# Modulation in small chunks beside the projection, with partial sums kept on chip

## The chip, the cores and the metric

The kernel runs on one core of a Trainium2 chip. The metric is the device time of one execution in microseconds (us). An engine's name and its short form in the profile: TensorE (PE; PEld is its weight load), VectorE (DVE), ScalarE (ACT), GpSimd (POOL), SyncE (SP). A "q" behind it means its instruction queue, for instance where it issues a DMA.

## What is computed

One layer of a decoder trunk, for 256 prompt tokens and 8 x 8 sample tokens, 320 in all, with model width 4096, in 32-bit floats:

```
mod = c @ w_ada + b_ada                      # 4096 x 12288, 9 rows of c
shift, scale, gate = jnp.split(mod, 3, axis=-1)
h = _rmsnorm(x, g_norm) * (1.0 + scale[:, None]) + shift[:, None]
proj = h @ w_in                              # 4096 x 10240
a_b, a_c, a_x, a_g, b_x, b_g, c_u, c_g = _split_cols(proj)
...
mixed = jnp.concatenate([out_a, out_b, out_c], axis=-1) @ w_out   # 4096 x 4096
x = x + gate[:, None] * mixed
```

out_a is a short gated convolution of 1024 channels. out_b (2048 channels) is a convolution of b_x, two gates from small matmuls, a recurrence in time and a gate from b_g. out_c (1024 channels) is a complex diagonal state space model on c_u (S5, in 8 units of 4 tiles), a GLU and a gate from c_g. A final RMSNorm follows. The states after the last token are outputs too.

## The kernel before

Activations lie transposed: 128 channels on the partitions, 320 tokens in the free dimension, 32 such tiles for h. Each large weight comes as slabs of 512 KB. A main slab holds two blocks of 128 rows by 512 columns. SyncE loads it (RAW, a ring of four), ScalarE rounds it to w_hi (L529), VectorE takes the rest, w_lo (L833), and TensorE multiplies: for four column blocks and two row blocks three matmuls with h_hi or h_lo, 24 in all (L375 to L377). A group of 512 output columns fills the four banks of the PSUM tensor M and is then read out. Weights are split three slabs ahead of use (AHEAD).

The modulation product goes the other way round: c (32 columns, 9 of them used) is the stationary operand and a slab of w_ada streams past it. A slab has two matmuls of 512 columns, recorded as four; each goes to another strip of 32 output partitions (r = 32 * (k % 4)). The four strips are partial sums, so ScalarE copies them out (acc_copy), and four matmuls with a selection matrix add them and turn them (ada_sum, L401).

The order of the work is written out by hand, engine by engine, with semaphores:

- First stage. ScalarE loads x whole, then the sum of squares is made (L853, L386). Shift and scale of four chunks of 512 channels follow, 128 modulation slabs from a ring of eight (L393, ada_ring). VectorE makes the normalised and modulated rows h (h_tmp, h_rows), four tiles a chunk.
- Folded stage (N_P = 8 groups of 8 main slabs, the lower half of the contraction). Before every main slab stand two modulation slabs of the other four chunks (ada_ring_x, a ring of four), and an ada_sum behind every eighth. The half sums of six groups go through ScalarE to DRAM (part_b, part_c), those of the last two to SBUF.
- U stage (N_U = 4 groups of 8 slabs): the upper half for c_u and c_g, added on VectorE.
- A stage (8 groups of 16 slabs) for the short convolution; beside it runs the S5 recurrence, on all engines, one unit a group.
- G stage: 8 slabs of the GLU.
- B stage: four times the upper half of b_x (8 slabs), then b_g (16 slabs), with the recurrence beside it (the gates' matmuls at L481).
- O stage: 8 output groups of 16 slabs. Gate modulation is folded in, two slabs after eight of the main slabs of each group (L499), then a sum (L507) behind slab 13. SyncE issues main and gate slabs in turn (L338, L340). At a group's end ScalarE copies out, VectorE adds gate times output to x (L1164 to L1167), ScalarE squares (L804), VectorE adds the squares (L1171).
- Tail: the sum of squares over partitions (L511), root, reciprocal (L1179), x times 1/rms times weight on VectorE (L1184) and, for two of eight groups, GpSimd and ScalarE (L1313, L815); y goes out as 5 MB.

The tables for S5 (T0, 14 rows of 1064) are computed whole on VectorE and ScalarE in the first stage.

## Time and profile before

| | |
|---|---|
| median of three runs | 2138.58 us (2137.79 to 2139.91) |
| the profiled execution | 2137.69 us, its span 2136.1 us |
| TensorE busy, weight load | 94%, 81% |
| VectorE, ScalarE, GpSimd busy | 49%, 37%, 20% |
| DMA | 473.88 MB, 222 GB/s over the span |
| chain that ended last | PE 74%, POOL 7%, DMA 7%, issue 5%, DVE 4% |

The span is the time from the first instruction to the last; what lies around it is in the execution's own time alone. Busy is the time with an instruction under way. Matmuls are pipelined and their ends are modelled, so the distance of starts says what one costs, not its length. A window's row gives the busy time with the number of instructions for PE, PEld, DVE, ACT and POOL in this order, then PEclk, the share of TensorE's full clock that was granted, the busy share of the DMA engines and GB/s. In a timeline's row the bracket tells how long the engine was idle before it and what ended that.

### The profile page before, as it was taken

How to read it: one execution, taken by the hardware profiler on the slowest of the kernel's cores; microseconds unless marked ns; L12 is line 12 of the kernel's file. 1: busy time of each engine (PE TensorE's matmuls, PEld its weight loads, DVE VectorE, ACT ScalarE, POOL GpSimd, SP SyncE). 2: the span in 40 equal slices, each digit the busy share in tenths (PEclk: the TensorE clock that was granted, in tenths of full speed). 3: DMA queues.
4: the chain of work that ended last, by engine and by line, in shares of the span. 5: the costliest groups of instructions: out<-in, count | busy, mean ns of one | idle time of the engine just before them, and what ended most of it. 6: DMA issues, size and time to landing. Idle time of an engine off the chain costs nothing.

```text
span 2136.1 us, 36787 instructions
## 1 busy us (share of the span) xinstructions
PE 2007.3 (94%) x13066; PEld 1724.2 (81%) x13066; DVE 1051.4 (49%) x1324; ACT 800.7 (37%) x1075; POOL 434.3 (20%) x501
## 2 busy tenths in 40 slices
PE   2887999999999998999989999999999999999994
PEld 0111777778999997989979999999988888888883
DVE  4812233233447677676777455565653333333334
ACT  3001223233334444444435445646563323333232
POOL 0000000000107765867658101000000000000001
PEclk9999999999999999999999999999999999999997
DMA  7999999997543433334333444454457787666862
GB/s 311 410 410 385 334 339 348 344 332 291 172 144 127 133 127 117 129 120 141 123 126 130 161 147 165 134 173 154 155 216 259 261 318 258 249 247 246 306 234 98
DMA packets 129149, 473.88 MB, mean 222 GB/s; under 512 B 14640, under 2 KB 15472, under 8 KB 128960
## 3 DMA queue, kind: packets, MB, share of 16 engines
q1 hardware_dynamic: 122256, 445.70, 58.1%
q0 software_dynamic: 4816, 18.10, 2.5%
q10 hardware_dynamic: 2016, 9.42, 1.1%
q8 instruction: 19, 0.31, 0.1%
q14 instruction: 42, 0.34, 0.1%
HBM read 463.09 MB, written 10.07 MB: 222 GB/s over the span
## 4 chain that ended last, share of the span: by engine, by line
PE 74%; POOL 7%; DMA 7%; issue 5%; DVE 4%; ACTq 1%; ACT 1%; POOLq 0%; SPq 0%; DVEq 0%
PE m L375 22%; PE m L377 21%; PE m L376 21%; DMA ada_ring<-in_ada 6%; PE aux L393 4%; PE aux L499 3%; POOL s_tmpp L1260 1%; POOL s_tmpp L1257 1%; PE aux L481 1%; DVE x L1184 1%; POOL cos L1218 1%; POOL s_h__105 L1256 1%; POOL sin L1216 1%; DMA ada_ring_x<-in_ada 1%; DVE w_lo L833 1%
## 5 line engine op out<-in xcount | busy, mean ns | idle before, releaser
L375 PE MATMUL m<-h_hi,w_hi 128*128 128x320 f32 x3584 | 1131.8, 316 | 4.7 <-DVE w_lo L833 4.6
L377 PE MATMUL m<-h_hi,w_lo 128*128 128x320 f32 x3584 | 1109.4, 310 | 0.0
L376 PE MATMUL m<-h_lo,w_hi 128*128 128x320 f32 x3584 | 1109.0, 309 | 0.0
L833 DVE TENSOR_TENSOR w_lo<-w_raw,w_hi 128x1024 fp32r<-128x1024 f32 x456 | 577.4, 1278 | 838.4 <-ACT w_hi L529 837.3
L529 ACT ACTIVATE w_hi<-w_raw 128x1024 fp32r<-128x1024 f32 x456 | 478.9, 1056 | 903.2 <-PE m L377 577.5
L375 PEld LDWEIGHTS m<-h_hi,w_hi 128*128 128x128 f32 x3584 | 674.9, 188 | 130.9 <-issue 113.6
L376 PEld LDWEIGHTS m<-h_lo,w_hi 128*128 128x128 f32 x3584 | 675.5, 188 | 0.8
L377 PEld LDWEIGHTS m<-h_hi,w_lo 128*128 128x128 f32 x3584 | 675.0, 188 | 0.0
L393 PE MATMUL aux<-ada_ring,c_T 128*32 128x512 f32 x512 | 123.8, 620 | 24.3 <-DMA ada_ring<-in_ada 24.3
L393 PEld LDWEIGHTS aux<-ada_ring,c_T 128*32 128x32 f32 x512 | 17.7, 110 | 124.2 <-DMA ada_ring<-in_ada 120.1
L393 PE MATMUL aux<-ada_ring_x,c_T 128*32 128x512 f32 x512 | 70.8, 612 | 3.6 <-DMA ada_ring_x<-in_ada 3.6
L1226 POOL DMA_DIRECT2D part_b<-part_b x4 | 2.4, 588 | 339.0 <-ACT part_b L605 339.0
L499 PE MATMUL aux<-gate_ring,c_T 128*32 128x512 f32 x512 | 69.2, 605 | 2.0 <-DMA gate_ring<-in_ada 2.0
L1309 POOL DMA_DIRECT2D x<-in_x x8 | 4.2, 531 | 312.9 <-PE m L377 312.9
L1313 POOL TENSOR_TENSOR x<-x,rstd 128x320 f32<-128x320 f32 x8 | 8.6, 1111 | 225.5 <-DVE rstd L1179 225.5
L1300 POOL COPY stage_h<-lru_r 128x18 f32<-128x18 f32 x8 | 4.9, 616 | 240.7 <-DVE lru_r L1094 240.7
L576 ACT ACTIVATE ada_acc<-aux 128x512 f32<-128x512 f32 x16 | 9.5, 595 | 117.0 <-PE aux L393 116.9
L1256 POOL TENSOR_TENSOR s_h__104<-q,cos 128x328 f32<-128x328 f32 x16 | 19.7, 1232 | 156.0 <-DVE q L1007 156.0
L1219 POOL TENSOR_TENSOR sin<-sin,cos 128x328 f32<-128x328 f32 x34 | 45.9, 1349 | 6.0 <-POOL cos L1218 5.9
L628 ACT ACTIVATE cos<-sin 128x328 f32<-128x328 f32 x33 | 15.6, 473 | 68.4 <-POOL sin L1219 68.3
L386 PE MATMUL aux<-x_sqa,sel_ones 128*128 128x320 f32 x8 | 4.6, 757 | 37.4 <-DVE x_sqa L853 37.4
L1260 POOL TENSOR_TENSOR s_tmpp<-q,cos 128x328 f32<-128x328 f32 x32 | 37.8, 1180 | 0.0
(237 smaller groups left out, 1507.6 us busy)
## 6 DMA issues: line engine op xcount, KB each, us to landing
w_raw<-in_w SPq DMA_DIRECT2D x456, 512.0 KB, 4.3
ada_ring<-in_ada SPq DMA_DIRECT2D x128, 512.0 KB, 9.0
ada_ring_x<-in_ada SPq DMA_DIRECT2D x128, 512.0 KB, 5.9
gate_ring<-in_ada SPq DMA_DIRECT2D x128, 512.0 KB, 5.7
x<-in_x ACTq DMA_DIRECT2D x1, 5120.0 KB, 16.6
x<-in_x POOLq DMA_DIRECT2D x8, 640.0 KB, 5.3
out_y<-x SPq DMA_DIRECT2D x7, 640.0 KB, 3.0
part_b<-part_b POOLq DMA_DIRECT2D x4, 688.0 KB, 6.5
```

Source lines behind the costliest of these rows:

```text
L375: mm(out, w_hi, hi[:, k, :], start=k == k0, stop=False)
L376: mm(out, w_hi, lo[:, k, :], start=False, stop=False)
L377: last = mm(out, w_lo, hi[:, k, :], start=False, stop=k == k0 + nk - 1)
L393: last = mm(A0[part][r:r + 32, :], CT[:, k, :], slot[:, kk, :], start=k < 4, stop=k >= KT - 4)
L481: last = mm(A0[2 * w + hd][:, 0:XW], WG[:, 2 * pr + hd, w, :], XB[:, 2 * pr + hd, :], start=True, stop=True)
L499: last = mm(A0[0][r:r + 32, :], CT[:, k, :], ADA2[:, n % RING, kk, :], start=k < 4, stop=k >= KT - 4)
L529: fn(W_HI[:, c % RING], RAW[:, c % RING].rearrange("p (k n) -> p k n", k=2), ACT.Copy).then_inc(w_hi_done, 1)
L833: tt(W_LO[:, c % RING], RAW[:, c % RING].rearrange("p (k n) -> p k n", k=2), W_HI[:, c % RING].bitcast(F32), SUB).then_inc(w_lo_done, 1)
L1184: last = stt(X[:, k, :], X[:, k, :], col(C_GF + k), RST2[:], MUL, MUL)
L1219: tt(sin, sin, cos, SUB).then_inc(frac_done, 1)
L1256: tt(hr, qr, cos, MUL)
L1260: then(tt(TMPP[:], qi, cos, MUL))
```

## The change

The modulation is cut into nine chunks of 32 slabs. Eight hold shift and scale for 512 channels each, the ninth the first quarter of the gate. A slab now is one block of 128 rows by 1024 columns, as four matmuls of 256 columns, one per output strip, all with the same stationary operand (recorded as eight). Each strip holds finished sums, so a VectorE transpose from PSUM takes the place of the copy and the selection matmuls, and the PSUM banks alternate between chunks.

Only chunk 0 stands before the first main slab, and TensorE does 24 of its slabs before the sum of squares. x comes in eight pieces and is kept where h_lo will be. The modulation slabs of the other eight chunks (256) are folded in four at a time behind every second main slab, at places that pairs_after gives: behind n = -3, -1, 1, 3, 4, 6, 8, 10, 11, 13 and so on, eight times in fourteen slabs. Their ring has six slots for the first 32 slabs and then four.

The head is now 14 half groups (seven groups of 512 columns: b_x of three, c_u, c_g) over eight steps of the contraction, 112 slabs of four row blocks by 256 columns. After each slab the sums go from PSUM to SBUF: copied by ScalarE in the first step, added by VectorE in the other seven. b_x of the three groups goes to DRAM at the end of the head and comes back in the B stage, which has 80 slabs instead of 96. The U stage is gone. S5 tables are made in four batches during the first four steps.

In the O stage gate modulation for two groups at a time is folded in, two slabs behind every second main slab, over the first six groups; TensorE waits for gmod_done at the start of groups 0, 2 and 4. ScalarE multiplies x by the final norm's weight after each group. The last group is read from PSUM by VectorE bank by bank, and the final product is ten wide operations on VectorE, with the root's table loaded early by a dummy operation.

```diff
-ADA_J = 8
-ADA_1 = ADA_J // 2
+HC, HK = 256, 4
+HGROUPS, HSTEPS = 7, 8
+HSL = 2 * HGROUPS
+N_H = HSL * HSTEPS
+CHUNKS = 9
+CW = 256
...
+        pairs_after = {n: [q for q in range(128) if (q | 1) * HSL // 16 - 3 == n] for n in range(-3, N_H)}
+
+        def ada_place(n):
+
+            if n < KT:
+                return n % 6, n // 6 + 1, n - 5
+            m = n % RING
+            first = KT + m
+            return m, len(range(m, KT, 6)) + (n - first) // RING + 1, (
+                n - RING + 1 if n >= first + RING else max(range(m, KT, 6)) + 1)
...
+            for n in range(-3, N_H):
+                if n in (HSL - 2, 2 * HSL - 2, 3 * HSL - 2):
+                    s5_batch((n + 2) // HSL)
+                for q in pairs_after[n]:
+                    for m in (KT + RING + 2 * q, KT + RING + 2 * q + 1):
+                        if m < CHUNKS * KT:
+                            ada_in(m)
+                if RING <= n + 6 < N_H:
+                    w_in(n + 6)
...
+            def ada_slab(n, bank):
+
+                slot, landed, _ = ada_place(n)
+                pe.wait_ge(ada_landed[slot], 16 * landed)
+                k = n % KT
+                for r in range(4):
+                    last = mm(A0[bank][32 * r:32 * r + 32, 0:CW], CT[:, k, :], ADAX[slot][:, r, :], start=k == 0,
+                              stop=k == KT - 1)
+                last.then_inc(ada_used, 1)
...
+            def head_slab(n):
+
+                st_, l, s_ = n // HSL, n % HSL, n % RING
+                pe.wait_ge(w_lo_done, n + 1)
+                if l == 0:
+                    pe.wait_ge(h_lo_done, st_ + 1 + 1)
+                if 2 <= n < HSL + 2:
+                    pe.wait_ge(hda_free, n - 2 + 1)
+                if n >= HSL + 2:
+                    pe.wait_ge(hdv_free, n - 2 - HSL + 1)
...
+            pe.wait_ge(c_in, 16)
+            for n in range(24):
+                ada_slab(n, 0)
             pe.wait_ge(sqa_done, 8)
...
+            for n in range(24, KT):
+                ada_slab(n, 0)
+            for n in range(-3, 0):
+                pairs(n)
+            for n in range(N_H):
+                head_slab(n)
+                pairs(n)
...
+            with pe.Fori(0, 3) as p:
+                k = 0
+                pe.wait_ge(gmod_done, p + 1 + 1)
+                for jj in range(2):
+                    for c in group_o(2 * p + jj):
+                        if c not in ((1, 3, 5, 7, 9, 11, 13, 15) if jj else (2, 4, 6, 8, 10, 12, 14, 15)):
+                            continue
...
+            def sums(n):
+
+                dve.wait_ge(slab_done, n + 1 + 1)
...
+                row, few = head_place(n)
+                bk = 2 * (n % 2)
+                tt(row, row, M[:, bk:bk + 2, 0:TP], ADD)
+                tt(few, few, MS[:, bk:bk + 2], ADD).then_inc(hdv_free, 1)
...
+            with dve.Fori(0, 3) as p:
+                st.enter(p, 2)
+                for odd in range(2):
+                    group_o(2 * p + odd, odd, False)
+                dve.wait_ge(gate_used, KT * (p + 1))
+                nc.vector.transpose(MODT2[:].rearrange("p b n -> p (b n)"), A0[0][:, 0:CW]).then_inc(gate_t_done, 1)
+                dve.wait_ge(gate_t_done, p + 1)
+                tt(MODG[:], MODT2[:, :, 0:9], PAR[:, bass.ds(C_BADA + 72 + 8 * p, 8)].unsqueeze(2).to_broadcast(
+                    [P, 8, 9]), ADD).then_inc(gmod_done, 1)
```

## Rows read from the trace of the kernel before

**Rows 1.** Windows by stage: length, busy us (xinstructions), clock, DMA share, GB/s

```profile
0.00:211.27 211.27, 139.46 (x592) 28.39 (x592) 83.94 (x119) 32.41 (x33) 1.45 (x5) 0.98 0.96 380
211.27:519.47 308.20, 308.20 (x2106) 244.06 (x2105) 97.35 (x108) 90.05 (x140) 9.54 (x11) 1.00 0.94 338
519.47:632.45 112.98, 112.98 (x770) 112.71 (x770) 51.43 (x70) 37.51 (x38) 9.37 (x16) 1.00 0.48 165
632.45:1179.10 546.65, 522.97 (x3394) 489.87 (x3392) 385.56 (x514) 247.19 (x372) 377.39 (x407) 0.98 0.38 127
1179.10:1209.97 30.87, 30.86 (x192) 30.87 (x193) 13.17 (x12) 13.62 (x18) 1.08 (x2) 0.93 0.41 143
1209.97:1566.34 356.37, 356.37 (x2371) 350.02 (x2369) 202.25 (x255) 201.99 (x259) 21.87 (x42) 1.00 0.45 153
1566.34:2103.35 537.01, 535.02 (x3650) 467.77 (x3648) 195.12 (x214) 169.45 (x203) 5.00 (x10) 1.00 0.71 256
2103.35:2136.10 32.75, 1.45 (x3) 0.50 (x2) 22.58 (x35) 8.51 (x15) 8.62 (x8) 0.58 0.40 160
```

**Rows 2.** Timeline of TensorE, first stage: start, us, engine, line, what, xcount [idle]

```profile
155.69 1.05 PE L393 MATMUL aux<-ada_ring,c_T 128*32 128x512 f32 x4 [0.23 <-DMA ada_ring<-in_ada]
156.98 1.05 PE L393 MATMUL aux<-ada_ring,c_T 128*32 128x512 f32 x4 [0.24 <-DMA ada_ring<-in_ada]
```

**Rows 3.** Timeline of TensorE, folded stage

```profile
216.19 1.06 PE L393 MATMUL aux<-ada_ring_x,c_T 128*32 128x512 f32 x8
...
220.90 1.07 PE L393 MATMUL aux<-ada_ring_x,c_T 128*32 128x512 f32 x8
```

**Rows 4.** Timeline of TensorE, A stage: matmuls with 32 output columns

```profile
760.51 0.46 PE L457 MATMUL aux<-s_h__104,s_cc 128*32 128x328 f32 x1
...
760.81 0.44 PE L457 MATMUL aux<-s_h__104,s_cc 128*32 128x328 f32 x1
```

**Rows 5.** Timeline of TensorE, start of the kernel

```profile
41.97 4.27 PE L393 MATMUL aux<-ada_ring,c_T 128*32 128x512 f32 x32
...
47.07 1.05 PE L393 MATMUL aux<-ada_ring,c_T 128*32 128x512 f32 x4 [0.83 <-DMA ada_ring<-in_ada]
...
52.35 1.05 PE L393 MATMUL aux<-ada_ring,c_T 128*32 128x512 f32 x4 [0.23 <-DMA ada_ring<-in_ada]
```

**Rows 6.** Timeline of SyncE's queue, same stretch

```profile
43.86 15.19 SPq L303 DMA_DIRECT2D ada_ring<-in_ada  x16
```

**Rows 7.** Timeline of VectorE at the first stage's end

```profile
208.16 1.38 DVE L939 TENSOR_SCALAR h_tmp<-h_tmp,mod 128x256 f32<-128x256 f32 x4
```

**Rows 8.** Timeline of TensorE, folded stage: a sum step, and one long burst

```profile
249.05 0.95 PE L401 MATMUL aux<-sel_ones,ada_acc 128*128 128x9 f32 x8
249.93 1.06 PE L393 MATMUL aux<-ada_ring_x,c_T 128*32 128x512 f32 x8
...
259.35 1.55 PE L393 MATMUL aux<-ada_ring_x,c_T 128*32 128x512 f32 x8
```

**Rows 9.** Groups of instructions by line, VectorE: busy, mean ns, idle before

```profile
L833 DVE TENSOR_TENSOR w_lo<-w_raw,w_hi 128x1024 fp32r<-128x1024 f32 x456 | 577.4, 1278 | 838.4 <-ACT w_hi L529 837.3 <-DVE y_sqs L1149 0.2
...
L853 DVE TENSOR_TENSOR x_sqa<-x_sqa,x_sq 128x1280 f32<-128x1280 f32 x7 | 10.4, 1492 | 1.0 <-ACT x_sq L555 0.3
```

**Rows 10.** Timeline of SyncE's queue at the O stage's start

```profile
1572.03 1.76 SPq L334 DMA_DIRECT2D gate_ring<-in_ada  x4
```

**Rows 11.** Timeline of TensorE, same stretch

```profile
1575.34 1.05 PE L499 MATMUL aux<-gate_ring,c_T 128*32 128x512 f32 x4 [1.80 <-DMA gate_ring<-in_ada]
```

**Rows 12.** Timeline of VectorE at the end of the first output group

```profile
1636.95 1.67 DVE L1164 SCALAR_TENSOR_TENSOR x<-out_tmp,mod,x 128x256 f32 x4 [1.79 <-ACT out_tmp L800]
...
1640.24 2.28 DVE L1171 TENSOR_TENSOR y_sqs<-y_sqs,y_sq 128x320 f32<-128x320 f32 x4 [0.71 <-ACT y_sq L804]
```

**Rows 13.** Timeline of TensorE, tail

```profile
2109.31 1.43 PE L511 MATMUL aux<-y_sqs,sel_ones 128*128 128x320 f32 x2 [5.94 <-DVE y_sqs L1171]
```

**Rows 14.** Timeline of VectorE, tail

```profile
2113.52 16.03 DVE L1184 SCALAR_TENSOR_TENSOR x<-x,par,rstd 128x320 f32<-128x320 f32 x24
```

More of the change, by code:

```diff
@@ L322, in _, with ada_in @@
-            for n in range(RING):
-                sp.wait_ge(ada_used, 2 * first - 2 * RING + n + 1)
-                sp.dma_start(ADAX[:, n], a["ada"][2 * first - RING + n]).then_inc(adax_landed[n], 16)
-            with sp.Fori(N_P * SPH // RING, SLAB_O // RING + 1) as r:
+            sp.sem_inc(bank_free, BLK)
+            def ada_in(n):
+                slot, _, used = ada_place(n)
+                if used > 0:
+                    sp.wait_ge(ada_used, used)
+                sp.dma_start(ADAX[slot][:], a["ada"][n]).then_inc(ada_landed[slot], 16)
@@ new lines, in pairs @@
+            def pairs(n):
+                for q in pairs_after[n]:
+                    j = 1 + q // 16
+                    if q % 16 == 0 and j >= 2:
+                        pe.wait_ge(mod_done, j - 1)
+                    for m in (KT + 2 * q, KT + 2 * q + 1):
+                        ada_slab(m, j % 2)
+            def head_slab(n):
[7 more added lines that the diff above has]
+                    pe.wait_ge(hdv_free, n - 2 - HSL + 1)
+                for b in range(2):
+                    out = M[:, 2 * (n % 2) + b, 0:T]
+                    for kk in range(HK):
+                        k = HK * st_ + kk
+                        at_ = kk % 2 * HC + b * P
+                        w_hi = W_HI[:, s_, kk // 2, at_:at_ + P]
+                        w_lo = W_LO[:, s_, kk // 2, at_:at_ + P]
+                        mm(out, w_hi, H_HI[:, k, :], start=kk == 0, stop=False)
+                        mm(out, w_hi, H_LO[:, k, :], start=False, stop=False)
+                        last = mm(out, w_lo, H_HI[:, k, :], start=False, stop=kk == HK - 1)
+                last.then_inc(slab_done, 1)
@@ new lines, in _ @@
+            h_hi(0)
+            for n in range(N_H):
+                st_, l = n // HSL, n % HSL
+                if 1 <= n <= HSL:
+                    first_sums(n - 1)
+                if n == 0:
+                    act.wait_ge(ada_used, KT)
+                hi(0, n + AHEAD, first=n + AHEAD < RING)
+                if l == 11 and st_ < HSTEPS - 1:
+                    h_hi(st_ + 1)
+                if st_ < 4:
+                    s5_part(st_, l)
+                if n == 4 * HSL + 2:
+                    act.wait_ge(sp_in, 1)
+                    fn(NEG8SP[:], NEG8SP[:], ACT.Exp).then_inc(sp_exp, 1)
@@ L967, in bank_ready @@
+            sums(N_H - 1)
             def bank_ready(q, b, nb_next):
@@ L1178, in _ @@
+            st.leave(3)
+            dve.wait_ge(gmod_done, 5)
+            group_o(6, 0, False)
+            group_o(7, 1, True)
             dve.wait_ge(yroot, 1)
```

925 lines of the change are left out of this document (444 added, 481 removed).

## The prediction

> **What bounds the kernel now.** Read the windows by stage first [rows 1]. TensorE is busy over the whole span except in the first stage, where 211.27 us pass before the first main matmul and DMA is busy 96% of the time. So one question per stage: which wait ends last.
>
> In that first stage each modulation slab (512 KB) costs 1.28 us from start to start (156.98 - 155.69), of which TensorE works 1.05 [rows 2], and the bracket names the DMA: the stage is DMA bound. From 519.47 to 632.45 TensorE does 32 main slabs and nothing else in 112.98 us [rows 1], so a main slab costs 3.53 us, at full granted clock (1.00) and 48% DMA. Between 211.27 and 519.47 a main slab and two modulation slabs take 220.90 - 216.19 = 4.71 us [rows 3]: two folded modulation slabs cost 1.18 us, 0.59 each, under half of what a slab costs alone. Every later stage is main slabs at 3.53 plus small extras; DMA is at 38 to 71% [rows 1]. The kernel is thus TensorE bound after a DMA-bound head.
>
> **The cost of a burst.** 32-column matmuls run side by side on different output strips. Eight matmuls of 328 columns start in four pairs about 0.28 us apart, the first at 760.51, the second at 760.81 [rows 4], that is 0.84 ns a column. A burst of two slabs is eight matmuls of 512 columns, four strips wide: two rounds of 0.43, 0.86 us; the rest of 1.18, 0.32 us, is entering and leaving the narrow shape. After the change a slab is eight matmuls of 256 columns, two rounds of 0.215. A burst of four slabs: 8 x 0.215 + 0.32 = 2.04 us (two bursts now: 2.36); a burst of two: 4 x 0.215 + 0.32 = 1.18, as now. No row shows 256-column rounds. From below the bound is this; from above it is a price per instruction: the fastest stream in the trace is four matmuls and four weight loads per 0.43 us, so a round could cost 0.43 whatever its columns. I take 0.215, since the 328-column rounds scale with columns, and keep the other end as a rival.
>
> The Trainium skill (TensorE: Matmul & The Clock Gate, Back-to-back issue gap) gives a stream of weight load and matmul pairs about 81 ns a pair at N=128. By that a round of four would be at least 0.32 us, and the sum below 76 us longer, about 2128. No row decides it.
>
> **Start, 211.27 to 77.** Before: four chunks (128 slabs) pass at 1.28 us, and TensorE takes the first at 41.97, after the sum of squares; SyncE refills only from 43.86 [rows 5, 6]. After: one chunk (32 slabs) and two bursts of four (8) precede the first main slab, and TensorE takes 24 slabs before it asks for the squares. The bytes set it, at 1.28 us per 512 KB: 40 modulation slabs 51.2, four main slabs 5.1, x 12.8, c 1.3, small tables 1.4, first S5 batch 1.7: 73.5. Data flows from about 2.4 us; the last landing and half a burst add about 1. So 77. The vector chain (transpose, four rows, copy, subtract) hides behind the last eight slabs: slab 31 lands near 65 and the chain takes about 8 (four row operations take 1.38 us [rows 7]; two more, the copy, the subtraction and the small ones about 4.5). If that cover failed it would cost single us.
>
> **Head, 77 to 625.** 112 main slabs x 3.53 = 395.4. 64 bursts less the two before it: 62 x 2.04 = 126.5. The eight sum steps at 0.88 us (249.05 to 249.93) [rows 8] go; a DVE transpose takes their place beside TensorE. DMA: 46 slabs of 512 KB for each 14 main ones are 58.9 us, plus 1.7 for an S5 batch, against 49.4 + 16.3 = 65.7 of TensorE: not the bound on average. But the ring holds four slabs, exactly one burst. Four loads issued from idle arrive over 8.5 us (issue from 43.86, the first taken at 47.07, the fourth at 52.35) [rows 5, 6]; the first is issued 0.9 after the burst begins, so the fourth lands at 9.4. With two main slabs between bursts the fourth is wanted at 9.1 + 1.3 = 10.4: covered by 1 us. The schedule puts one main slab between bursts twice per fourteen (after slabs 3 and 4, and 10 and 11): there it is wanted at 5.6 + 1.3 = 6.9, and up to 2.5 us are missing. 15 such places: 0 (loads closer than from idle) to 38; I take 1.5 each, 22. What is late next there is nothing: main weights are six slabs ahead in SyncE's order. The head is written out rather than looped, so its code is all new to the engine; the one odd burst in the folded stage now, 1.55 us instead of 1.06 [rows 8], may be such a fetch. Some 40 fetches, one in four at 0.5: 5. Bounds 0 and 20. Sum 395.4 + 126.5 + 22 + 5 = 549, less 1 for slab pitch at 3.52; end 625.
>
> Other engines in the head: per main slab VectorE has 1.28 (w_lo) [rows 9] and about 1 for sums into SBUF; every 14th also about 5 for rows and h_lo. In a slab of 3.53 plus its share of a burst this fits, and TensorE's wait for the sums two slabs back has a whole slab of slack. The S5 tables move there in four batches, three or four operations a slab, with table loads on ScalarE. GpSimd's three writes and two mask loads finish before its first table for the next stage. I cost these at nothing, cover 3.5 us a slab; below zero they can't go.
>
> **S5 and GLU stages** keep their code: 546.65 [rows 1] and 30.9 (1179.1 to 1209.97). End 1202.5.
>
> **Recurrent stage** loses sixteen main slabs that the head now has: 356.37 - 16 x 3.53 = 299.9. Gate weights and padded rows are wanted by slab 5, 21 us in; their loads and small copies take about 13, an estimate. End 1502.4.
>
> **Output stage, 537.01 to 524.** 128 x 3.53 = 451.8. Modulation: 96 slabs in 48 bursts of two instead of 64: 56.6 instead of 75.5. The eight sum steps (7) go. At the start TensorE waits today until 1575.34 for gate slabs issued at 1572.03 [rows 10, 11], 3 us over all; the burst moves one slab back and that wait goes, but the fifth main slab, queued on SyncE behind four gate loads, is late next: 2. SyncE alternates a main load with a gate load that waits for a used slot; consumption now trails one slab per slab, so main loads leave two slabs and two bursts ahead of use, 9.2 us, against 9.1 for landing, split and subtraction: 0 to 10, taken 0. The added wait is TensorE's for gmod_done at the head of groups 2 and 4. VectorE does the transpose behind the whole residual of the group before: it starts at 1636.95 and ends its squares at 1640.24 + 2.28 = 1642.52 [rows 12], 6.4 us after the group's last matmul; transpose and add 0.8. TensorE has one burst, 1.2, to hide it. Everything of TensorE stands behind it, then the weight rings. 6.0 idle twice. After the 3.6 us pause before 211.27 the first main slab takes 4.92 (to 216.19) where others take 3.71 [rows 1, 3], so 1.2 more for each restart: 14.4. Today the same product is wanted at slab 13 of a group and hides. Sum 451.8 + 56.6 + 2 + 14.4, less 1: 524. End 2026.4.
>
> **Tail, 32.75 to 23.** The last group is read straight from PSUM a bank at a time. The squares end about 2.4 us after the last matmul, against 6 (the sum's matmul starts at 2109.31) [rows 13]; sum 1.4, root 0.5 with its table already loaded, reciprocal 2.15: about 7 instead of 10.1 (2113.52 [rows 14]). Then VectorE's 16.03 us in 24 operations [rows 14] become ten wide ones; 1280 elements take 1.49 [rows 9], under 12 in all, so the transfer of 5120 KB (12.8) with 3 for issue and landing sets the end. End 2049.3.
>
> **Against the run:** the profiled execution took 2137.69 with a span of 2136.1, 1.6 around it, and the median is 0.9 above. 2049.3 + 1.6 + 0.9 = 2052.
>
> **Rivals.** (a) *Price per instruction, the slower side.* After 77 us there are 62 x 8 + 48 x 4 = 688 rounds. If a round costs 0.43 instead of 0.215, 148 us come on top: 2200. It decides from 0.34 us a round (86.6 / 688 = 0.126 above). For it: twice the matmuls for the same bytes, and no row of a denser stream. Against: inside a round starts lie a few ns apart, and a queue filled during main matmuls may carry a burst. 0.05 for over 0.34, 0.08 for a part of it, 2112 to 2134. (b) *The ring starves in every burst.* The cover of 1 us fails through fetches, S5 batches or GpSimd's writes: 0.7 us x 62 = 43: 2095; 0.14. (c) *The two doubtful waits aren't there*: ring waits 0, fetches 0, and the gate product early enough: 22 + 5 + 10 less: 2015. 0.12. (d) *The change doesn't shorten the head*, because DMA sets it: 415 slab equivalents x 1.28 + 2.4 = 534, below 625, so this needs a rate a sixth lower than now; 0.01, and then about the time of before.
>
> **Numbers.** Forecast case 2052 (2030 to 2075) 0.60. The range of 0.8: 2018 to 2112, which takes in most of (b) and of (c). Faster by over 0.2% (what a measurement of this kernel can tell from no change) 0.94, within it 0.01, slower 0.05.
>
> **What would show it.** First main matmul at 77, not above 85; bursts of four slabs 2.04 from start to the next main matmul's start less 0.1; waits for the modulation ring only where one main slab lies between bursts; a main slab 3.53 throughout; two gaps of 6 us at the third and fifth output group; last stage 23. A burst over 3 us makes (a) true. Idle time before every burst makes (b) true.

## The result, and the profile after

| | before | after |
|---|---|---|
| median | 2138.47 us (2137.79 to 2139.91, 4 runs) | 2118.14 us (2114.31 to 2124.14, 4 runs) |
| ratio | | 0.9907, 95% interval 0.9882 to 0.9931 |
| profiled execution, its span | 2137.69 us, 2136.1 us | 2114.31 us, 2112.7 us |

The change makes the kernel faster by 0.9%, where 4.0% was forecast; 2118 lies outside the range of 2018 to 2112. The profiled execution is the fastest of the four. The stages are cut at the starts of TensorE's first main matmul of each. Windows by stage of the kernel after (same columns as [rows 1]):

```profile
0.00:83.19 83.19, 42.24 (x329) 9.78 (x329) 25.77 (x28) 20.50 (x20) 8.26 (x9) 0.87 0.96 373
83.19:655.89 572.70, 541.58 (x4677) 456.53 (x4673) 307.82 (x511) 159.13 (x187) 10.43 (x18) 0.98 0.89 339
655.89:1204.81 548.92, 524.06 (x3394) 491.44 (x3393) 389.29 (x512) 248.38 (x376) 377.45 (x408) 0.98 0.38 126
1204.81:1235.07 30.26, 30.26 (x193) 30.26 (x194) 13.16 (x12) 13.17 (x17) 1.08 (x2) 0.95 0.44 146
1235.07:1535.12 300.05, 300.05 (x1986) 293.68 (x1985) 175.04 (x207) 186.84 (x251) 18.57 (x41) 1.00 0.45 152
1535.12:2089.74 554.62, 519.20 (x3842) 481.07 (x3840) 197.71 (x220) 177.44 (x224) 5.02 (x10) 0.96 0.63 218
2089.74:2112.73 22.99, 1.59 (x4) 0.50 (x2) 16.11 (x20) 3.27 (x7) 0.00 (x0) 0.55 0.57 228
```

Set beside the forecast, stage by stage:

| stage | forecast | measured | off by |
|---|---|---|---|
| start | 77 | 83.2 | +6.2 |
| head | 548 | 572.7 | +24.7 |
| S5 (A) and GLU (G) | 577.5 | 579.2 | +1.7 |
| recurrent (B) | 299.9 | 300.05 | +0.2 |
| output (O) | 524 | 554.6 | +30.6 |
| tail | 23 | 22.99 | 0 |

So 63 us of the span are missing, and 55 of them in two stages: the head and the output stage. The recurrent stage and the tail came out to 0.2 us. In the two bad stages the window rows already hint at what happened: TensorE is busy 519.20 of 554.62 us in the output stage and the granted clock is 0.96, where the stage before it has 300.05 of 300.05 at 1.00. TensorE stood still, and was slower behind it.

Who made it stand, from the waits, the two rows of the output stage first, then the one of the head (engine and line waited for: us in total, times, longest):

```profile
PE m L411 <- DVE mod_gate L1251: 17.6, 2, 8.9
PE m L411 <- ACT out_tmp L846: 14.9, 3, 5.3
...
PE aux L425 <- DMA ada<-in_ada: 31.1, 41, 2.4
```

The first was forecast (12 us in 2). The second was not: ScalarE's copy of a finished output group out of PSUM was never named as a risk. The third was forecast at 22 us.

**The head.** A burst of four modulation slabs, the main slab behind it, and then the next burst, which has only one main slab between it and the first. Timeline of TensorE, main matmuls left out:

```profile
171.00 1.93 PE L425 MATMUL aux<-ada,c_T 128*32 128x256 f32 x32
172.86 0.41 PE L455 MATMUL m<-h_hi,w_hi 128*128 128x320 f32 x1
...
176.58 1.07 PE L425 MATMUL aux<-ada,c_T 128*32 128x256 f32 x16
178.96 0.64 PE L425 MATMUL aux<-ada,c_T 128*32 128x256 f32 x8 [1.31 <-DMA ada<-in_ada]
180.20 0.91 PE L425 MATMUL aux<-ada,c_T 128*32 128x256 f32 x8 [0.61 <-DMA ada<-in_ada]
181.04 0.64 PE L455 MATMUL m<-h_hi,w_hi 128*128 128x320 f32 x1
```

The clean burst is one row: 32 matmuls in 1.93 us. The close one is in three pieces: two slabs are there, the third and fourth are taken as they land. The pieces last 1.07 + 0.64 + 0.91 = 2.62 us together (the third partly at a lower clock, 0.72 from 180 to 181), so a broken burst also costs TensorE more work, besides the 1.92 us that it stands still. SyncE's queue in the same stretch:

```profile
171.69 1.75 SPq L326 DMA_DIRECT2D ada<-in_ada  x4
173.49 0.50 SPq L332 DMA_DIRECT2D w_raw<-in_w  x1
177.28 4.20 SPq L326 DMA_DIRECT2D ada<-in_ada  x4
```

The four slabs of the second burst are the four issued from 171.69 on, as the first burst frees their slots. From the first issue to the fourth slab taken pass 180.20 - 171.69 = 8.51 us. At the start of the kernel before it was 52.35 - 43.86 = 8.49 us [rows 5, 6]: the same row that the prediction had read. Part of the lateness may be the DMA's rate: a close place uses up five slabs of 512 KB (one main, four modulation) in 5.58 us, and at 1.28 us each they are 6.4 us of transfer. From 171.70 to 180.20 the DMA was busy 92% of the time and moved 351 GB/s. Behind the place TensorE's clock fell as well:

```profile
180.00:184.00 4.00, 3.80 (x19) 3.12 (x20) 0.00 (x0) 0.00 (x0) 0.00 (x0) 0.57 1.01 410
```

**The output stage, behind an odd group.** At the end of the first group (and of the third and fifth) the last two gate bursts stand one main slab apart. TensorE's second burst and the next main slab, SyncE's loads, ScalarE's splits:

```profile
1602.80 1.07 PE L556 MATMUL aux<-gate_ring,c_T 128*32 128x256 f32 x16
1608.54 0.64 PE L411 MATMUL m<-h_hi,w_hi 128*128 128x320 f32 x1 [4.66 <-ACT out_tmp L846]
```

```profile
1598.93 0.33 SPq L377 DMA_DIRECT2D gate_ring<-in_ada  x1
...
1600.70 0.33 SPq L375 DMA_DIRECT2D w_raw<-in_w  x1
```

```profile
1607.10 1.06 ACT L582 ACTIVATE w_hi<-w_raw 128x1024 fp32r<-128x1024 f32 x1 [1.49 <-DMA w_raw<-in_w]
1608.06 1.07 ACT L846 ACTIVATE out_tmp<-m 128x320 f32<-128x320 f32 x3
```

Read it backwards. TensorE waits for ScalarE to empty PSUM (L846, 1608.06). ScalarE works in order, and ahead of that copy stands the split of a later main slab (L582, 1607.10), which waits for its load. That load is the one at 1600.70, the last of four that follow each other by 0.59 us; the first of them, a gate load at 1598.93, had waited until the burst before had used up its slot. So a gate slab's slot delays a main load, that holds ScalarE, and ScalarE holds TensorE, for the sake of a slab that is split ahead of its use. Right behind the wait TensorE runs at its lower clock:

```profile
1608.50:1612.00 3.50, 3.46 (x13) 3.47 (x14) 3.12 (x7) 0.96 (x3) 0.00 (x0) 0.50 1.00 407
```

**The output stage, behind an even group.** TensorE's one burst behind the second group and the slab after it, and VectorE in the same stretch:

```profile
1675.87 1.07 PE L556 MATMUL aux<-gate_ring,c_T 128*32 128x256 f32 x16
1685.62 0.63 PE L411 MATMUL m<-h_hi,w_hi 128*128 128x320 f32 x1 [8.69 <-DVE mod_gate L1251]
```

```profile
1677.62 1.23 DVE L879 TENSOR_TENSOR w_lo<-w_raw,w_hi 128x1024 fp32r<-128x1024 f32 x1 [1.84 <-ACT w_hi L582]
1679.06 1.67 DVE L1237 SCALAR_TENSOR_TENSOR x<-out_tmp,mod_gate,x 128x256 f32 x4 [0.21 <-ACT out_tmp L846]
...
1682.35 2.28 DVE L1216 TENSOR_TENSOR y_sqs<-y_sqs,y_sq 128x320 f32<-128x320 f32 x4 [0.71 <-ACT y_sq L852]
1684.54 0.44 DVE L1249 STREAM_TRANSPOSE gate_t<-aux 128x256 f32<-128x256 f32 x1
```

This is the forecast wait: the gate product is turned behind the whole residual and the squares. But it takes 8.7 us instead of 6.0, because a late main slab's subtraction (1677.62) stands ahead of the residual.

**The start.** SyncE's queue:

```profile
57.80 10.34 SPq L326 DMA_DIRECT2D ada<-in_ada  x6
68.18 0.43 SPq L339 DMA_DIRECT2D s_tmp<-in_rep  x1
...
71.43 0.91 SPq L343 DMA_DIRECT2D s_tmp<-in_s5b  x2
72.38 3.49 SPq L326 DMA_DIRECT2D ada<-in_ada  x4
```

Eight small S5 table loads take SyncE from 68.18 to 72.34 at about 0.5 us each, with modulation slabs behind them that the second burst is waiting for.

### The profile page after: what moved, and what is told of

Read it like the earlier page. It is cut to its first block, busy times and chain, and to the rows that moved or that the text cites. A ratio compares the mean times of both kernels' runs of the same rounds, so it can differ in the third digit from the quotient of the medians.

```text
span 2112.7 us, 37786 instructions
## 1 busy us (share of the span) xinstructions
PE 1959.0 (93%) x14410; PEld 1763.3 (83%) x14410; DVE 1124.9 (53%) x1507; ACT 808.7 (38%) x1080; POOL 420.8 (20%) x487
## 4 chain that ended last, share of the span: by engine, by line
PE 68%; DMA 11%; POOL 8%; issue 5%; DVE 5%; ACT 1%; SPq 1%; POOLq 0%; DVEq 0%; ACTq 0%
PE m L411 15%; PE m L413 14%; PE m L412 14%; DMA ada<-in_ada 9%; PE m L455 6%; PE m L456 5%; PE m L457 5%; PE aux L425 5%; DMA w_raw<-in_w 2%; PE aux L556 2%; POOL s_tmpp L1332 1%; POOL s_tmpp L1335 1%; PE aux L519 1%; DVE w_lo L879 1%; POOL sin L1292 1%
## 5 line engine op out<-in xcount | busy, mean ns | idle before, releaser
L411 PE MATMUL m<-h_hi,w_hi 128*128 128x320 f32 x2688 | 850.9, 317 | 40.2 <-DVE mod_gate L1251 17.6
L582 ACT ACTIVATE w_hi<-w_raw 128x1024 fp32r<-128x1024 f32 x456 | 479.1, 1056 | 963.0 <-DMA w_raw<-in_w 393.5
L411 PEld LDWEIGHTS m<-h_hi,w_hi 128*128 128x128 f32 x2688 | 511.1, 190 | 77.9 <-issue 43.1
L412 PEld LDWEIGHTS m<-h_lo,w_hi 128*128 128x128 f32 x2688 | 511.4, 190 | 0.8
L413 PEld LDWEIGHTS m<-h_hi,w_lo 128*128 128x128 f32 x2688 | 511.1, 190 | 0.0
L425 PE MATMUL aux<-ada,c_T 128*32 128x256 f32 x2304 | 170.1, 416 | 72.1 <-DMA ada<-in_ada 72.0
L455 PEld LDWEIGHTS m<-h_hi,w_hi 128*128 128x128 f32 x896 | 171.5, 191 | 28.5 <-issue 28.5
L425 PEld LDWEIGHTS aux<-ada,c_T 128*32 128x32 f32 x2304 | 61.7, 113 | 159.3 <-DMA ada<-in_ada 113.2
L456 PEld LDWEIGHTS m<-h_lo,w_hi 128*128 128x128 f32 x896 | 171.6, 191 | 0.0
L457 PEld LDWEIGHTS m<-h_hi,w_lo 128*128 128x128 f32 x896 | 171.3, 191 | 0.0
L940 DVE TENSOR_TENSOR b_x<-b_x,m 128x512 f32<-128x512 f32 x42 | 28.8, 685 | 85.8 <-PE m L457 70.1
L556 PE MATMUL aux<-gate_ring,c_T 128*32 128x256 f32 x768 | 51.4, 385 | 0.0
```

The source lines that it names most:

```text
L411: mm(out, w_hi, hi[:, k, :], start=k == 0, stop=False)
L412: mm(out, w_hi, lo[:, k, :], start=False, stop=False)
L413: last = mm(out, w_lo, hi[:, k, :], start=False, stop=k == nk - 1)
L425: last = mm(A0[bank][32 * r:32 * r + 32, 0:CW], CT[:, k, :], ADAX[slot][:, r, :], start=k == 0, stop=k == KT - 1)
L455: mm(out, w_hi, H_HI[:, k, :], start=kk == 0, stop=False)
L456: mm(out, w_hi, H_LO[:, k, :], start=False, stop=False)
```

## The experiments

Every kernel is the one after with the edits named. Times are medians of 4 runs (9 for one of them); stage lengths are from its profiled execution and are cut as above; line numbers differ from those of after by up to 12 where lines were added. The kernel before, run beside them, had 2137.28, 2139.42, 2136.93 and 2136.55 us in the four sets. Two executions of one kernel can differ by more than a stage's last microseconds: after itself lies between 2114.31 and 2124.14 us, so a difference of 1 to 3 us in a stage is that of two single executions and no more.

### Main loads ahead of the gate waits

```
+ def main_in(i, slot):
+     sp.wait_ge(w_lo_done, SLAB_O + i - RING + 1)
+     sp.dma_start(RAW[:, slot], a["w"][SLAB_O + i]).then_inc(w_landed[slot], 16)
+ for n in range(2):
+     main_in(RING + n, n)
  with sp.Fori(0, 3 * KT // RING - 1) as r:
      for n in range(RING):
-         sp.wait_ge(w_lo_done, SLAB_O + r * RING + n + 1)
-         sp.dma_start(RAW[:, n], a["w"][SLAB_O + (r + 1) * RING + n]).then_inc(w_landed[n], 16)
+         main_in((r + 1) * RING + n + 2, (n + 2) % RING)
          sp.wait_ge(gate_used, r * RING + n + 1)
          sp.dma_start(ADA2[:, n], a["ada"][first + (r + 1) * RING + n]).then_inc(gate_landed[n], 16)
...
```

The loop over the main slabs that are left is moved on by the same two slabs.

> The kernel after, with SyncE's order in the output stage changed alone: the load of a main slab is issued two slabs ahead of where it stood, so that it no longer stands behind the wait for a gate slab to be used up (gate_used). Theory (queue order): in the kernel after, the first main slab behind the second gate burst of each group came late (starts 5.04 to 5.68 us behind the burst instead of 1.0, and the slab behind it took 6.1 us instead of 3.6), because SyncE issued its load only at the end of the burst; with the load ahead, the three gaps of some 5 us go, the waits of TensorE's L411 rounds for ScalarE's out_tmp (14.9 us in 3) fall to under 3 us, the output stage falls from 554.6 us by 16 to 24 us, and the time from 2118 to 2094 to 2102 us. Rival (clock and burst length set it: the burst of four ends at a lower granted clock whatever the loads do): the stage stays within 4 us of 554.6. Rival (DMA rate): the gate loads move later by what the main loads gain, the waits turn into waits for gate slabs of the same sum, and the stage stays within 4 us.

Measured: 2091.87 us (2079.21 to 2095.64, the widest of these kernels), 0.9776 of before (0.9735 to 0.9817). Window of the output stage, and all that is left of the two waits there (the line numbers are shifted by 7):

```profile
1535.42:2064.14 528.72, 513.17 (x3842) 475.33 (x3840) 197.44 (x220) 178.27 (x224) 5.00 (x10) 0.99 0.65 229
```

```profile
PE m L418 <- DVE mod_gate L1258: 12.5, 2, 6.3
```

The stage lost 25.9 us, a little more than expected. The wait for out_tmp is gone, not small: queue order on SyncE was its whole cause. Neither rival holds: the bursts are as long as before, and the DMA rate went up to 229 GB/s. The gmod wait also fell, from 17.6 to 12.5 us in two, 6.25 each.

### The gate product in two PSUM banks in turn

```
- with pe.Fori(0, 3) as p:
+ for p in range(3):
      k = 0
-     pe.wait_ge(gmod_done, p + 1 + 1)
+     if p != 1:
+         pe.wait_ge(gmod_done, 1 + 1 + p // 2)
...
- last = mm(A0[0][32 * r:32 * r + 32, 0:CW], CT[:, k, :], ADA2[:, k % RING, r, :],
+ last = mm(A0[p % 2][32 * r:32 * r + 32, 0:CW], CT[:, k, :], ADA2[:, k % RING, r, :],
...
```

VectorE turns the product out of the same bank, A0[p % 2].

> The kernel after, with the gate product of the three groups written to two PSUM banks in turn, so that the gate bursts behind groups 1 and 3 no longer wait for VectorE to have read the previous gate product (gmod_done). All else is as in the kernel after, SyncE's order too. Theory: the two waits (17.6 us in 2 in the profile after, where the prediction had 7.2 each) lie in front of a second loss at the same place: the main slab behind those bursts has its load issued as late as at the other boundaries. So of the 10.4 us that each of the two boundaries loses, some 3 us go, and the stage falls from 554.6 by 4 to 8 us; TensorE's wait for ScalarE's out_tmp appears at all five boundaries instead of three. Rival (the bank alone costs all of it): both boundaries become clean, 18 to 21 us go, and the time falls to some 2098 us.

Measured: 2098.06 us, 0.9808 (0.9790 to 0.9827), and in its trace:

```profile
1540.86:2076.93 536.07, 514.72 (x3842) 476.71 (x3840) 197.50 (x220) 177.24 (x224) 5.00 (x10) 0.98 0.63 226
```

```profile
PE m L411 <- ACT out_tmp L847: 18.4, 5, 5.6
```

The stage lost 18.5 us: the rival was right. The wait for out_tmp does now show at five boundaries as the theory said, but the two new ones are only 1.91 and 0.73 us long. The mistake was to carry what happens at the end of odd groups over to even ones. The last two bursts of an even group stand two main slabs apart (1667.63 and 1675.87 us in the kernel after), not one, so the load behind them is hardly late.

### Both

> Both edits in one kernel: the main loads ahead of the gate waits and the gate product in two banks in turn. Theory: all five boundaries become clean (first main slab 1 to 2 us behind each burst, no wait of L411 above 2 us for either), and the output stage falls from 554.6 us to 518 to 524 us, which is what the prediction had without its two gmod waits (524 less 14.4 plus 1 to 9 for the loads); the time is 2080 to 2088 us. Rival (the two are not independent, the DMA queue then bounds the stage): less than the sum of the two single edits by over 5 us, with waits for gate slabs in its place.

Measured: 2073.57 us, 0.9701 (0.9684 to 0.9717). Output stage:

```profile
1538.39:2049.44 511.05, 508.15 (x3842) 470.47 (x3840) 197.14 (x220) 178.32 (x224) 5.00 (x10) 1.00 0.66 237
```

The stage fell by 43.6 us, against 25.9 + 18.5 = 44.4 for the two alone: they add. It ends 7 us below the 518 to 524 that was expected, but the sum given for that range, 524 less 14.4 plus 1 to 9, comes to 510.6 to 518.6, and 511.05 lies in it. The row settles how the loss was made up. TensorE's idle time was 17.6 + 14.9 = 32.5 us; its busy time went from 519.20 to 508.15, 11.1 us less for the same 3842 matmuls, as the granted clock went from 0.96 to 1.00. The gate matmuls take 51.39 us in both kernels, so the slower work was the main matmuls' (474.02 us against 463.39). Together 43.6. A quarter of the price of these waits was paid after they ended.

### Modulation bursts of two in the head

```
- pairs_after = {n: [q for q in range(128) if (q | 1) * HSL // 16 - 3 == n] for n in range(-3, N_H)}
+ pairs_after = {n: [q for q in range(128) if q * HSL // 16 - 3 == n] for n in range(-3, N_H)}
```

> The kernel after, with the modulation slabs of the head folded two at a time behind fourteen main slabs in each of the eight steps, instead of four at a time behind seven. The work and the number of loads are the same; only the length of the bursts differs. Theory (latency of a ring of four): in the kernel after the ring is emptied by each burst, and where only one main slab lies between two bursts (3.6 us), the fourth slab has not landed: those intervals are 7.2 to 9.1 us instead of 5.5, and the slab behind is then slower by 1.2 us. With bursts of two the ring never empties, TensorE's waits for modulation slabs (31.1 us in 41) fall below 5 us, and of the head's 572.7 us some 45 us go, while 48 more switches between the two kinds of work cost 0.33 us each, 16 us: the head is 540 to 550 us and the time 2088 to 2097 us. Rival (the DMA rate sets the head: 339 GB/s at 0.89 busy): waits are only spread out, their sum stays over 20 us, and the head is 570 to 590 us. Rival (the price of a burst is in the switches): the head gets longer, to 590 us or more.

Measured: 2119.21 us, 0.9909 (0.9893 to 0.9926), the time of after. Window and wait of the head, and a burst in it:

```profile
83.37:661.83 578.46, 552.82 (x4677) 449.68 (x4673) 308.61 (x511) 158.99 (x187) 10.46 (x18) 0.98 0.92 336
```

```profile
PE aux L425 <- DMA ada<-in_ada: 25.4, 29, 2.5
```

```profile
180.46 1.07 PE L425 MATMUL aux<-ada,c_T 128*32 128x256 f32 x16
181.76 0.64 PE L425 MATMUL aux<-ada,c_T 128*32 128x256 f32 x8 [0.22 <-DMA ada<-in_ada]
184.39 0.64 PE L425 MATMUL aux<-ada,c_T 128*32 128x256 f32 x8 [2.00 <-DMA ada<-in_ada]
```

The waits fell by 5.7 us and TensorE's busy time rose by 11.2, the entering and leaving of 48 more bursts. Every number of the theory missed, and the first rival's came true (waits over 20 us, head 570 to 590). That does not yet make the DMA's rate the cause, for the run keeps the close places: sixteen pairs over fourteen main slabs put two pairs behind the same slab twice in a step, and the rows show one of these. Four slabs are wanted there at once, one main slab behind the last pair, and the loss is that of the kernel after.

### Half the bytes for each modulation load

```
- sp.dma_start(ADAX[slot][:], a["ada"][n]).then_inc(ada_landed[slot], 16)
+ if n < KT + RING:
+     sp.dma_start(ADAX[slot][:], a["ada"][n]).then_inc(ada_landed[slot], 16)
+ else:
+     sp.dma_start(ADAX[slot][:, 0:2], a["ada"][n][:, 0:2]).then_inc(ada_landed[slot], 16)
```

> The kernel after, with the head's modulation slabs from number 36 on loaded by half: 256 KB instead of 512 KB each, so that half of each slab is what an earlier load left there and the shifts and scales are not the reference's. Instructions, waits and order on every engine are unchanged; only the bytes differ. The run with pairs instead of bursts of four left TensorE's waits for modulation slabs where they were (two of its sixteen places per step still fold four slabs), so it did not tell the length of a load apart from the switch. Theory (a ring of four cannot cover the 5 to 8 us that a load takes when 1.28 us of transfer stand behind each of those before it): with half the bytes the intervals at the close places fall from 7.2 to 9.1 us to 5.5, the slab behind them is no longer slower, TensorE's waits for modulation slabs (31.1 us) fall below 5, the head falls from 572.7 us by 40 to 50 and the time to 2068 to 2080 us. Rival (switches and clock: a second burst after one main slab is dear by itself): the intervals stay over 7 us and the head falls by under 10 us.

Measured: 2072.07 us, 0.9687 (0.9670 to 0.9704). The head:

```profile
81.19:611.72 530.53, 527.08 (x4677) 452.02 (x4673) 308.18 (x511) 159.18 (x187) 9.60 (x18) 1.00 0.73 244
```

```profile
PE aux L428 <- DMA ada<-in_ada: 3.1, 3, 1.7
```

The head fell by 42.2 us with not one instruction changed. Again the two rows make the sum: 31.1 - 3.1 = 28.0 us of waits, and 541.58 - 527.08 = 14.5 of busy time. The clock (1.00 instead of 0.98) is only a part of the second. The main matmuls take 412.32 us instead of 418.78, 6.5 less. The modulation matmuls take 123.50 instead of 131.39, 7.9 less, and those are mostly bursts no longer broken into pieces: the kernel with leftover pairs below has a clock of 1.00 too, 40 waits, and 130.40 us of them.

So the close places cost what they do because the loads arrive late, and the second burst is not dear by itself. Why the loads are late this run can't say: half the bytes shorten each load and also take over a quarter of its traffic off the DMA (339 to 244 GB/s). The length of a load and the DMA's rate are not told apart.

### Slot order of the start, and the S5 batch behind it

```
- m = n % RING;  first = KT + m
+ m = (n - KT + 2) % RING;  first = KT + (m - 2) % RING
```

> The kernel after, with the order of ring slots at its start changed: modulation slab 32 goes to slot 2 instead of slot 0, so that SyncE waits for slabs folded earlier (26 and 27) instead of slab 30. In the kernel after SyncE stood at slab 32 until 65.6 us and the queue ran empty twice (66 to 72 and 76 to 78 us); the first main slab began at 83.2 us instead of the predicted 77. Theory (the slot order holds the start): the first main slab begins 3 to 6 us earlier and the head keeps its length, so the time falls by 3 to 6 us. Rival (the sum step and the transposes behind slab 31 set the start, loads come early enough): the first main slab stays within 1 us of 83.2.

Measured: 2119.00 us, 0.9913 (0.9895 to 0.9931); first main slab at 81.41 us. Eight kernels here whose start is that of after have it between 81.19 and 84.34, so 1.8 us earlier is no effect that can be told. The second kernel keeps this edit and adds one:

```
- s5_batch(0)
  for n in range(-3, N_H):
+     if n == -2:
+         s5_batch(0)
```

> The kernel after, with the slot order of the start as in the run before (slab 32 to slot 2) and the first batch of S5 tables issued by SyncE behind the loads of slabs 36 to 39 instead of ahead of them. With the slots alone the first main slab began at 81.4 us instead of 83.2, while two runs that left the start as it was had 81.2 and 82.4; so the slots were worth little: the eight small S5 loads then stood at 67.9 to 71.2 us in front of slab 36, whose load landed only at 76.4. Theory (SyncE's queue in the start): both out of the way, the burst behind slab 35 runs without a gap of over 2 us and the first main slab begins at 76 to 79 us; the time falls by 3 to 6 us against after. Rival (the VectorE chain or the loads' bytes set the start): 81 to 83 us as before. What could be lost: ScalarE waits for the tables in front of its fifth weight slab, up to 3 us in the first step.

Measured: 2111.64 us, 0.9879 (0.9860 to 0.9898), first main slab at 78.84. SyncE's queue now runs ten modulation loads through, then the tables:

```profile
57.91 15.80 SPq L326 DMA_DIRECT2D ada<-in_ada  x10
73.75 0.43 SPq L339 DMA_DIRECT2D s_tmp<-in_rep  x1
```

The three kernels with both edits have 78.84, 79.42 and 79.56, all below the range of the others. They are 3.6 to 4.4 us earlier than after, some two thirds of the 6.2, by both edits of SyncE's order together. Against the two kernels with the slots alone (81.41 and 81.92, the second below) the tables make 1.9 to 3.1 of it. The eight table loads, 1.7 us of data by the prediction's count, hold SyncE's queue for 4.2. The tables' move without the slots was not run, and the rest is open.

### Leftover pairs between the bursts of four

```
+ after_slab = [0, 0, 2, 2, 3, 4, 4, 6, 6, 8, 8, 10, 10, 11, 12, 12]
- pairs_after = {n: [q for q in range(128) if (q | 1) * HSL // 16 - 3 == n] for n in range(-3, N_H)}
+ pairs_after = {n: [q for q in range(128) if q // 16 * HSL + after_slab[q % 16] - 3 == n]
+                for n in range(-3, N_H)}
```

> The kernel after, with the head's bursts laid out otherwise over the fourteen main slabs of a step: bursts of four behind every second main slab throughout (seven of them), and the two pairs that are left over each behind one of the main slabs between. In the kernel after eight bursts of four stand behind fourteen main slabs, so twice in a step two of them have only one main slab between, and there the intervals are 7.2 to 9.1 us instead of 5.5. Theory (four slots and 5 to 8 us of latency): a pair needs only two of the four slots refilled, and the burst of four behind it finds two waiting, so each close place loses 0.5 to 1.5 us instead of 3; 16 more switches cost 5 us; the head falls from 572.7 us by 15 to 30 us and the time from 2118 to 2090 to 2103 us. Rival (DMA rate): the same bytes per step, so the head stays at 570 to 580 us with the waits elsewhere.

Measured: 2104.75 us, 0.9844 (0.9828 to 0.9861).

```profile
82.42:642.97 560.55, 534.85 (x4676) 448.40 (x4673) 307.14 (x511) 159.65 (x187) 9.26 (x15) 1.00 0.92 347
```

```profile
PE aux L427 <- DMA ada<-in_ada: 25.4, 40, 1.7
```

The head fell by 12.2 us, under the 15 to 30 expected but well clear of the rival. Waits are only 5.7 us less, in as many pieces, but none is over 1.7 us, and with them the clock is at 1.00: busy time fell by 6.7 although each step has one more burst. (The expectation counted 16 more switches; there are 8.) The same bytes now flow at 347 GB/s instead of 339, so 339 was not what the DMA could do, though it was 0.92 busy.

### The main load behind the modulation loads at close places

```
+ if n > 0 and n + 5 < N_H and pairs_after[n - 1] and pairs_after[n]:
+     w_in(n + 5)
- if RING <= n + 6 < N_H:
+ if RING <= n + 6 < N_H and not (n >= 0 and pairs_after[n] and n + 1 < N_H and pairs_after[n + 1]):
      w_in(n + 6)
```

> The kernel after, with SyncE's order in the head changed at the close places alone: where bursts of four stand behind two main slabs in a row, the load of a main weight slab that lay between their eight modulation loads is issued behind all of them. The main slab is wanted six slabs later, so nothing should miss it. Theory (what TensorE waits for is the transfer that stands ahead of the last slabs of the second burst, 1.28 us for each 512 KB): each of the fifteen close places gets shorter by up to 1.28 us, more where the slab behind it was slowed as well, so the head falls from 572.7 us by 10 to 25 us and the time to 2093 to 2108 us. Rival (a fixed latency of 5 to 7 us from issue to landing, whatever stands ahead): no change, 570 to 575 us.

Measured: 2121.85 us (9 runs, 2117.66 to 2131.38), 0.9942 (0.9926 to 0.9958); head 578.62, no gain and rather a loss, though the ranges of the two kernels overlap. SyncE's queue and TensorE at a close place:

```profile
175.36 10.78 SPq L326 DMA_DIRECT2D ada<-in_ada  x8
186.19 1.39 SPq L332 DMA_DIRECT2D w_raw<-in_w  x3
```

```profile
180.24 1.07 PE L427 MATMUL aux<-ada,c_T 128*32 128x256 f32 x16
183.74 0.64 PE L427 MATMUL aux<-ada,c_T 128*32 128x256 f32 x8 [2.43 <-DMA ada<-in_ada]
```

The edit works as written: eight modulation loads in one run, the main loads after. But the second burst takes the first four of the eight, and the main load had stood behind those four in the kernel after as well (SyncE's rows of the head above: x4, then x1, then x4). What was moved stood ahead of nothing that was late. The expectation had the wrong load; that a latency which no bytes change sets the price does not follow either, since half the bytes took it away.

### All of them

> Four edits in one kernel: main loads ahead of the gate waits, the gate product in two banks in turn, the slot order of the start, and the head's leftover pairs between the bursts of four. The first two alone gave 2073.6 us together. Theory (each loss has its own place): the gains add, 15 to 30 us from the head and 3 to 6 us from the start, for 2040 to 2056 us, with the output stage at 511 us as before. Rival (the head is held by the DMA rate): 2066 to 2072 us.

Measured: 2055.58 us, 0.9608 (0.9592 to 0.9624): start 81.9, head 558.07, output stage 512.79. The gains add, as expected, but for the start.

> All edits in one kernel: main loads ahead of the gate waits, the gate product in two banks in turn, leftover pairs between the bursts of four, the start's slot order, the S5 batch later, and the main load behind the modulation loads at close places. All but the last two gave 2055.6 us, with the head at 558.1 us and the first main slab at 81.9. Theory: start 3 to 5 us shorter, head 8 to 15 us shorter, so 2036 to 2045 us. Rival (neither of the two does anything): 2053 to 2058 us.

Measured: 2063.33 us, 0.9651 (0.9634 to 0.9667): start 79.4, head 568.63. Worse than both theory and rival. Two edits had been added at once; one more kernel tells them apart:

> All edits but one: main loads ahead of the gate waits, the gate product in two banks in turn, leftover pairs between the bursts of four, the start's slot order and the S5 batch later; the main load stays where it was at the close places. The kernel with that move too took 2063.3 us (head 568.6), the one with neither it nor the S5 move 2055.6 (head 558.1, start 81.9). Theory (moving the main load did harm, since it only held back loads that the queue had room for, and helped no slab that was late): the head is back at 556 to 562 us, the start at 79 to 80, the time 2049 to 2056 us. Rival (the S5 batch inside the first steps does the harm): the head stays at 565 to 570 and the time at 2059 to 2065 us.

Measured: 2054.87 us, 0.9615 (0.9599 to 0.9631). The start is 79.56 us. The head:

```profile
79.56:639.50 559.94, 534.97 (x4676) 449.09 (x4673) 306.87 (x511) 160.40 (x190) 9.26 (x15) 1.00 0.92 348
```

The theory holds: without the moved main load the head is back at 560, so that move alone cost 8.7 us (8.5 in the medians). Why it does harm was argued in the expectation and is not shown. This kernel and the one without the S5 move (2055.58) can't be told apart in time; either is 3% faster than the kernel after, with the same modulation in chunks.

## Why the prediction was right and wrong, step by step

**Right.** The price of a burst, on which the main rival rested: the row x32 above lasts 1.93 us, the last matmul in it 0.38, so the seven rounds before the last start (1.93 - 0.38) / 7 = 0.22 us apart, against 0.215 taken and 0.43 feared. The whole price came out as well: bursts with two main slabs between them start 9.10 us apart (161.90 and 171.00), less 2 x 3.53 that is 2.04. A round does go by its columns; rival (a), the slower side, is refuted. The Trainium skill (TensorE: Matmul & The Clock Gate, Back-to-back issue gap) gives about 81 ns a pair at N=128, by which a round of four pairs is an estimate of 0.32 us. Here four pairs of 32 columns side by side took 0.22, 55 ns each, and the measurement decides. Right too: S5 and GLU stages, the recurrent stage and the tail (the reciprocal ends 7.0 us into it as forecast, the wide operations take 11.44 us, and the transfer ends last). The waits of the head sit where one main slab lies between bursts, 30.2 us of the 31.1, so rival (b) did not happen. Rivals (c) and (d) did not either. No run shows the 5 us for code fetches: in the head of after the undisturbed bursts are 9.09 to 9.11 us apart throughout.

**Start, +6.2.** The step counted bytes and found 77. It left out how long SyncE is held by small loads: eight S5 tables, 4 us of its queue, ahead of modulation slabs. Moving them and changing the slot order gave 3.6 to 4.4 us together, of which the tables are 1.9 to 3.1.

**Head, +24.7.** The step was right in its mechanism and its rows, and wrong in the value taken. It worked out that the fourth slab lands 2.5 us late (8.5 us for four loads from idle [rows 5, 6]), then took 1.5 each, hoping that loads would come closer than from idle. They took 8.51 us at the place shown, and TensorE stood still for 2.0 us a place on average. And it gave these waits no price beyond their own length: the broken bursts and the lower clock behind them, 14.5 us in all, had no term, though each wait for gmod_done had one. With half the bytes the whole term measured 42.2 us (28.0 idle, 14.5 more work), where 22 stood. The rest of the head is 530.5, against 395.4 + 126.5 - 1 + 5 = 525.9: 4.6 more, part of it waits that half the bytes left. Without the 5 for fetches, which nothing measured bears out, it would be 9.6 more, so it is by luck that this miss looks small. Sum 42.2 - 22 + 4.6 = 24.8.

The Trainium skill (DMA: Bandwidth & Descriptors, Anatomy of one DMA — SWDGE (gpsimd) path) fits a transfer issued from GpSimd as 2.0 us plus its bytes at 436 GB/s. By that four slabs of 512 KB issued together are an estimate of 6.8 us; SyncE's four took 8.5 both times, with other loads around them. By the estimate the fourth slab would land at 0.9 + 6.8 = 7.7 us, 0.8 later than wanted, 12 us over the fifteen places; the measured term was 42.2.

**Output stage, +30.6.** Three parts, from three runs:
- The clean stage is 511.05 us (both edits), against 524 - 14.4 = 509.6: +1.4.
- The gmod wait by itself, with the loads in time, is 528.72 - 511.05 = 17.7 for two, against 14.4: +3.3. Its idle part was right, 6.25 each against 6.0; the clock behind it was 2.5 each (513.17 - 508.15 over two), not 1.2.
- The alternation on SyncE is the step that failed: "9.2 us, against 9.1 for landing, split and subtraction: 0 to 10, taken 0". It cost 25.9. The sum had 0.1 us of slack and was made for the regular spacing of two main slabs a burst; at the odd boundaries there is one. The prediction knew that spacing, and used it in the head, but did not look for it here. And it followed a late main load only to its own use. It reached TensorE sooner, through ScalarE's queue, on a copy that had nothing to do with it.

1.4 + 3.3 + 25.9 = 30.6.

**Open.** The 24.5 us of waits that are left in the head of the best kernel: a fifth slot in the ring would end them if the ring is the cause, and less so if the DMA is, which is 0.92 busy there. It wasn't tried. Why a start with both its edits is still 1.8 to 2.6 us over the sum of bytes is not known.

## What to carry to other kernels

Where a term is worked out from a row and comes to 2.5, take 2.5; a milder value needs a row of its own. Where transfers are issued in turn from one queue, look at the place with the least work between two waits, not at the mean spacing, and follow a late load through every in-order engine that handles it: what is queued behind it there may be wanted first. When an engine's waits are costed, add the slower work that comes with them, here a quarter to a third of the whole: the lower clock behind a long wait, and the extra time of a burst that is taken in pieces.

## What the runs showed of the hardware

- The price of a stall goes on after it. In the output stage 32.5 us of waits went with 11.1 us of slower work (clock 0.96 against 1.00, and 0.50 for the 3.5 us behind one of them). In the head 28.0 went with 14.5, of which 6.5 are main matmuls (0.98 against 1.00) and 7.9 modulation matmuls, whose bursts were broken by the waits. How long the single wait is seems to matter: two heads have 25.4 us of waits each, one in 29 waits of up to 2.5 us with a clock of 0.98, the other in 40 of up to 1.7 with 1.00. That was seen, not tested.
- Four loads of 512 KB issued from SyncE into a short queue take 8.5 us until the last is used, in two kernels and at two places, though back to back each takes 1.28 us. In the second case a main load was issued right behind them, and the DMA moved 351 GB/s meanwhile.
- Small loads cost the issuing queue more than the DMA: eight table loads held SyncE for 4.2 us.
